# The norm between two transformer blocks folded into column factors and a row scale at evacuation; residual by column halves; last scaling shared by two engines

## The reference

```python
def rms_norm(x, g):            # first block; rms_norm_2 is the same with w
    return x * lax.rsqrt(jnp.mean(x * x, axis=-1, keepdims=True) + EPS) * g
...
x = even_layer(x, mem, ...)    # x + (y @ w_out)
x = odd_layer(x, mem, ...)     # x + (y @ w_out)
x = rms_norm(x, final_norm_g)  # end of the first block
for i in range(2):
    x = hybrid_layer(x, ...)   # h = rms_norm_2(x, norm_w[i]); ...; return x + merged @ w_out
return rms_norm_2(x, final_norm_w_2)
```

## Time and profile before

| | |
|---|---|
| median of 3 runs | 3183.61 us (3182.48 to 3185.02) |
| the profiled execution | 3181.94 us |
| its span, first to last instruction | 3179.9 us |
| PE busy | 3147.0 us, 99% |
| DVE busy | 1979.3 us, 62% |
| ACT busy | 1602.9 us, 50% |
| mean granted clock of TensorE | 0.997 |

### The profile page before, as it was taken

One profiled execution on the slowest core, in us unless ns is written; L12 is line 12 of the kernel. 1 busy time (PEld: TensorE's weight loads), 2 busy tenths in 40 slices (PEclk: granted clock), 3 DMA queues, 4 the chain that ended last, 5 costly groups with the idle time before them and its releaser, 6 DMA issues.

```text
span 3179.9 us, 38255 instructions
## 1 busy us (share of the span) xinstructions
PE 3147.0 (99%) x15096; PEld 2641.3 (83%) x15096; DVE 1979.3 (62%) x2980; ACT 1602.9 (50%) x2253; POOL 10.1 (0%) x22
## 2 busy tenths in 40 slices
PE   8999999999999999999999999999999999999998
PEld 7888888888987888888888888888888888888886
DVE  5555455565455699976555555558998655555554
ACT  7655454565454544555544444444555655444443
POOL 0000000000000000000000000000000000000000
PEclk9999999999999999999999999999999999999999
DMA  8555555545566555556566666565555466666664
GB/s 306 164 158 169 174 195 187 180 143 161 155 198 195 156 173 165 174 147 178 168 190 193 189 192 194 184 186 179 167 167 166 149 181 179 193 202 194 193 185 145
DMA packets 301442, 570.32 MB, mean 179 GB/s; under 512 B 18096, under 2 KB 36672, under 8 KB 300880
## 3 DMA queue, kind: packets, MB, share of 16 engines
q1 hardware_dynamic: 296800, 555.55, 58.2%
q10 hardware_dynamic: 3040, 6.41, 0.6%
q0 software_dynamic: 1424, 5.92, 0.5%
HBM read 565.72 MB, written 2.10 MB: 179 GB/s over the span
## 4 chain that ended last, share of the span: by engine, by line
PE 98%; DVE 1%; ACT 0%; DMA 0%; issue 0%; POOL 0%; DVEq 0%; SPq 0%
PE gp L108 90%; PE bk L108 5%; PE bk L111 3%; DVE X L139 0%; DMA raw<-in_ev_w_mem_kv 0%; DVE wl L134 0%; ACT gp L123 0%; DVE X L134 0%; DVE Hl L139 0%; ACT Yh L123 0%; DVE tmp L151 0%; ACT G L123 0%; DVE G L139 0%; ACT wh L123 0%; DVE st L134 0%
## 5 line engine op out<-in xcount | busy, mean ns | idle before, releaser
L134 DVE TENSOR_TENSOR wl<-raw,wh 128x1024 fp32r<-128x1024 f32 (+3 forms) x1088 | 1286.8, 1187 | 941.5 <-ACT wh L123 939.3
L123 ACT ACTIVATE wh<-raw 128x1024 fp32r<-128x1024 f32 (+3 forms) x1088 | 1121.4, 1034 | 1325.9 <-PE gp L108 1313.9
L108 PE MATMUL gp<-wh,Hh 128*128 128x512 f32 (+3 forms) x2400 | 925.3, 386 | 0.1
L108 PE MATMUL gp<-wh,Hl 128*128 128x512 f32 (+3 forms) x2400 | 911.9, 380 | 0.0
L108 PE MATMUL gp<-wl,Hh 128*128 128x512 f32 (+3 forms) x2400 | 911.2, 380 | 0.0
L108 PE MATMUL gp<-wh,Yh 128*128 128x512 f32 (+2 forms) x1952 | 762.0, 390 | 8.9 <-DVE wl L134 8.5
L108 PE MATMUL gp<-wh,Yl 128*128 128x512 f32 (+2 forms) x1952 | 755.2, 387 | 0.0
L108 PE MATMUL gp<-wl,Yh 128*128 128x512 f32 (+2 forms) x1952 | 754.8, 387 | 0.0
L108 PEld LDWEIGHTS gp<-wh,Hl 128*128 128x128 f32 x2400 | 451.2, 188 | 86.3
L108 PEld LDWEIGHTS gp<-wh,Hh 128*128 128x128 f32 x2400 | 451.6, 188 | 82.7 <-issue 1.3
L108 PEld LDWEIGHTS gp<-wl,Hh 128*128 128x128 f32 x2400 | 451.8, 188 | 81.3
(11 more groups left out here) (117 smaller groups left out, 1211.8 us busy)
## 6 DMA issues: line engine op xcount, KB each, us to landing
raw<-in_w_in SPq DMA_DIRECT2D x560, 512.0 KB, 3.7
raw<-in_ev_w_in SPq DMA_DIRECT2D x104, 512.0 KB, 3.8
raw<-in_od_w_in SPq DMA_DIRECT2D x80, 512.0 KB, 3.8
raw<-in_w_out SPq DMA_DIRECT2D x64, 512.0 KB, 4.7
raw<-in_ev_w_out SPq DMA_DIRECT2D x40, 512.0 KB, 3.7
raw<-in_od_w_out SPq DMA_DIRECT2D x36, 512.0 KB, 4.2
raw<-in_w_b_out SPq DMA_DIRECT2D x32, 512.0 KB, 4.6
raw<-in_w_a_out SPq DMA_DIRECT2D x32, 512.0 KB, 4.9
```

The lines of the kernel that those rows point to most:

```text
L108: return self.e.matmul(out, l, r, start=start, stop=stop)
L123: return self.e.activation(out, in_, func, **kw)
L134: return self.sketch(157 + size(a) * 1.042) if self.e is None else self.e.tensor_tensor(out, a, b, op)
```

## The change

Seven edits go together.

1. Between the blocks X is not scaled before it is used. The transposed blocks of layer 2 are made from X as the residual leaves it, part by part as for the other layers, with g·w as column factor (`gains` multiplies the two once).
2. The row scale of x2 is worked out from squares of x·g (`weigh` makes it in X) and from rs1, and `refine` multiplies rs1 into it; it acts at evacuation. `final_scale` of f0 multiplies X by rs1 later; the residual of layer 2 waits for it.
3. `residual` is two instructions of 256 columns in each row half; a `turn_in` waits for its half.
4. `mem_kv(1)` moves behind the `swkv` gemm.
5. At the end `weigh` writes X·g into M, part by part. The last scaling is a multiplication by the row scale alone: six pieces of 128x512 on DVE and two on ACT (`scale_out`).
6. Of the last part's two squares one goes to DVE (`square_last`), into `gp`, with the sum as accumulator.
7. The stores, in the order 2, 3, 0, 1, go through the queue of SP.

```diff
-         (("x", 3), 16))
+         (("x", 3), 16), (("f0",), 16))
@@ tables
-        mem_kv(1)
         W = I["od_w_in"][0]
         self.swkv = gemm(1, "H", 0, W, 1024, 256, 16, "swkv")
         roped(self.swkv, 0, 256, 64, rope_c)
         turned(self.swkv, self.swk, 0, 2)
+        mem_kv(1)
@@ sources
-            if n == 2:
-                return [self.v_fin.at((0, c))]
-            return [self.v_x.at(self.outs[n - 1][c].g)]
+            return [self.v_x.at((self.outs[n - 1][c].g, i % 4 // 2))]
@@ sp_program: store and stored moved here from pool_program
+        e.wait_ge(*P.v_fin.at((1, n)))
+        if n < 2:
+            e.wait_ge(*P.a_fin.at(n))
+        e.dma_start(o[:, :, c], P.M[:, :, c]).then_inc(*P.s_out[n].up("o", 16))
@@ act_program: in square_out
-        for t in range(2):
+        for t in range(1 if (gm.L, n) == (3, 3) else 2):
@@ act_program
+    def scale_out(n):
+        x = P.M[:, 1, 512 * n:512 * n + 512]
+        e.wait_ge(*P.v_rs.at("f1"))
+        e.wait_ge(*P.v_gf.at((1, n)))
+        e.activation(x, x, ACT.Copy, scale=P.rs[:, 1:2]).then_inc(*P.a_fin.up(n))
@@ dve_program: stat
+        if name == "x2":
+            w = P.st.buf(name)[:, 6:8]
+            e.wait_ge(*P.v_rs.at("f0"))
+            e.tensor_tensor(w, P.rs1, P.rs1, ALU.mult).then_inc(*P.v_stat.up((name, 2)))
+            e.wait_ge(*P.v_stat.at((name, 2)))
+            e.tensor_tensor(v, v, w, ALU.mult).then_inc(*P.v_stat.up((name, 3)))
@@ dve_program
-    def residual(g):
+    def residual(g, h):
...
-        x = P.X[:, :, 512 * n:512 * n + 512]
+        x = P.X[:, :, 512 * n + 256 * h:512 * n + 256 * h + 256]
...
+        if gm.L == 2:
+            e.wait_ge(*P.v_fin.at((0, n)))
+        e.tensor_tensor(x, P.gp[g % 2][:, :, 256 * h:256 * h + 256], x, ALU.add).then_inc(*P.v_x.up((g, h)))
+    def square_last(g):
+        x = P.X[:, 1, 1536:2048]
+        e.wait_ge(*P.v_x.at((g, 1)))
+        e.scalar_tensor_tensor(P.gp[g % 2][:, 1, :], x, 1.0, x, ALU.mult, ALU.mult,
+                               P.sum_x[:, 7:8]).then_inc(*P.v_sq.up(("f1", 3, 1)))
+    def weigh(f, n):
+        x, w = P.X[:, :, 512 * n:512 * n + 512], P.gfin[:, 512 * n:512 * n + 512].unsqueeze(1)
+        e.wait_ge(*P.s_gfin[f].at("g"))
+        e.wait_ge(*P.v_x.at((P.outs[1 + 2 * f][n].g, 1)))
+        if f:
+            to = P.M[:, :, 512 * n:512 * n + 512]
+            e.wait_ge(*P.p_in.at(("m", 1, 14)))
+        else:
+            to = x
+            e.wait_ge(*P.a_sq.at(("f0", n, 1)))
+            e.wait_ge(*P.p_in.at(("x", 2, 4 * n), ("x", 2, 4 * n + 2)))
+        e.tensor_tensor(to, x, w.broadcast_to([128, 2, 512]), ALU.mult).then_inc(*P.v_gf.up((f, n)))
@@ final_scale
-        for t in range(2):
-            i = e.scalar_tensor_tensor(P.X[:, t, c], P.X[:, t, c], P.rs[:, t:t + 1], P.gfin[:, c], ALU.mult, ALU.mult)
+        to, s = (P.M, P.rs) if f else (P.X, P.rs1)
+        for t in range(1 if f and n < 2 else 2):
+            i = e.tensor_scalar(to[:, t, c], to[:, t, c], s[:, t:t + 1], None, ALU.mult)
@@ add_steps
+            add("dve", "residual", g, 0)
+            add("dve", "residual", g, 1)
...
-            if gm.L in (0, 2):
+            if gm.L < 3:
...
-                for n in range(4):
+                for n in (2, 3, 0, 1):
+                    add("dve", "weigh", f, n)
+                    if not f:
+                        add("act", "square_in", "x2", n)
+                    elif n < 2:
+                        add("act", "scale_out", n)
+                if not f:
+                    norm("x2")
+                for n in (2, 3, 0, 1):
                     add("dve", "final_scale", f, n)
```

More of the change, by code:

```diff
@@ L674, in drained @@
         if gm.kind == "out":
+            if gm.L == 3 and gm.part == 3:
+                return self.v_sq.at(("f1", 3, 1))
             return self.a_sq.at((self.norm(gm.L), gm.part, 1))
@@ L810, in raw, with store, stored @@
         e.dma_start(P.raw[f % RAW][:, :, 0:gm.n], src).then_inc(*P.s_raw[f % RAW].up(f, 16))
-    return {"load_memt": load_memt, "load_mem2": load_mem2, "raw": raw}
+    def store(n):
+        o = P.out.rearrange("o (t p) c -> p (o t) c", p=128)
+        c = slice(512 * n, 512 * n + 512)
+        e.wait_ge(*P.v_fin.at((1, n)))
+        if n < 2:
+            e.wait_ge(*P.a_fin.at(n))
+        e.dma_start(o[:, :, c], P.M[:, :, c]).then_inc(*P.s_out[n].up("o", 16))
+    def stored(n):
+        e.behind("store", 1)
+        e.wait_ge(*P.s_out[n].at("o"))
+    return {"load_memt": load_memt, "load_mem2": load_mem2, "raw": raw, "store": store, "stored": stored}
 def pool_program(P, e):
@@ L853, in pad @@
         e.memset(P.glu[:, :, 0:30], 0.0).then_inc(*P.g_pad.up(l))
[L855 to L863, removed]
     return {"zero": zero, "load_constants": load_constants, "load_gfin": load_gfin, "load_second": load_second,
-            "load_cc": load_cc, "pad": pad, "store": store, "stored": stored}
+            "load_cc": load_cc, "pad": pad}
 def pe_program(P, e):
@@ L1237, in in_hi @@
             e.wait_ge(*P.s_gains.at("g"))
+            if of == ("x", 2):
+                e.wait_ge(*P.v_gains.at("x2"))
             c = P.gain_of(of) + i
@@ L1277, in root @@
         e.wait_ge(*P.v_stat.at((name, 1)))
[L1278 to L1281, removed]
+        if name in ("x1", "x2", "x3", "f1"):
+            e.wait_ge(*P.a_evac.at((P.h_end[("x1", "x2", "x3", "f1").index(name)].g, "end")))
         v = P.st.buf(name)[:, 4:6]
@@ L1400, in in_lo, with gains @@
             P.bank.give(key, P.v_in, key)
+    def gains():
+        a, b = P.gain[("x", 2)], P.gain[("f0",)]
+        e.wait_ge(*P.s_gains.at("g"))
+        e.tensor_tensor(P.gcols[:, a:a + 16], P.gcols[:, a:a + 16], P.gcols[:, b:b + 16],
+                        ALU.mult).then_inc(*P.v_gains.up("x2"))
     def stat(name):
@@ L1429, in refine @@
         i = e.tensor_tensor(out, out, t, ALU.mult)
+        if name == "x2":
+            i.then_inc(*P.v_rs.up((name, 4)))
+            e.wait_ge(*P.v_rs.at((name, 4)))
+            i = e.tensor_tensor(out, out, P.rs1, ALU.mult)
         if half is not None:
@@ L1718, in merge @@
         P.nat.give(gate, P.v_m, (g, 1))
-    def residual(g):
+    def residual(g, h):
         gm = P.gemms[g]
         n = gm.part
-        x = P.X[:, :, 512 * n:512 * n + 512]
+        if h:
+            e.behind("residual", g, 0)
+        x = P.X[:, :, 512 * n + 256 * h:512 * n + 256 * h + 256]
         e.wait_ge(*P.p_mm.at(gm.end))
@@ L1783, in add_steps @@
     add("act", "load_first")
+    add("dve", "gains")
     add("pool", "zero")
@@ L1825, in add_steps @@
                 add("pool", "load_gfin", f)
-                for n in range(4):
+                for n in (2, 3, 0, 1):
[4 more added lines that the diff above has]
+                        add("act", "scale_out", n)
+                if not f:
+                    norm("x2")
+                for n in (2, 3, 0, 1):
                     add("dve", "final_scale", f, n)
                     if f:
-                        add("pool", "store", n)
-                    else:
-                        add("act", "square_in", "x2", n)
+                        add("sp", "store", n)
                 if f:
                     for n in range(4):
-                        add("pool", "stored", n)
-                else:
-                    blocks(("x", 2), 16)
-                    norm("x2")
+                        add("sp", "stored", n)
             continue
```

48 lines of the change are left out of this document (30 added, 18 removed).

## The result

The median is 3168.17 us (3167.82 to 3168.6, 4 runs), against 3184.22 (3182.48 to 3185.02, 4 runs) for the kernel before on the same chip. That is 16.05 us less: ratio 0.995, 95% interval 0.9933 to 0.9968, so faster by more than the 0.2% that the prediction took as what can be told. The profiled execution took 3168.17 with a span of 3166.4 (before: 3181.94 and 3179.9).

The account below looks back on a forecast made before the run. PE bounds the kernel, busy 3147.0 of 3179.9 us, so only its stops and the tail count. Gains 9.2 + 2.0 + 0.6 = 11.8 us off 3183.61 give 3171.8 us, range 3168.5 to 3177.

Parts of the forecast that it names:

- The base: Starting time: the runs' median taken as 1.67 us above the profiled execution of 3181.94, so 3183.61 before the gain.
- block boundary: Stop between layers 1 and 2, about 1028 us: PE no longer waits for the scaled X, gain 9.2 us.
- inside the 9.2: At the stop between blocks, the transposes slowed by a granted clock of 0.70 were counted within the 9.2 us lost.
- The stores' queue: End of program: moving stores from POOL's queue to SP's gives between -1.5 and +0.7 us, taken as 0.3.
- first boundary: Between layers 0 and 1, about 553 us: reordering `mem_kv(1)` removes PE's stop of 2.05 us, taken as 2.0.
- rest of the tail: Tail apart from the queue: stores queued together fill the bandwidth, gain 0.3 us, bounds 0 and 0.5.
- rival C: Between layers 0 and 1: PE waits 2.6 us for late `mem` pieces and the 2.0 is not won; 3176.4, chance 0.12.
- E: Both boundaries: norm and operand work precedes weight splits in DVE's queue and PE starves 21.3 us; 3193.1, chance 0.03.
- D: Between the blocks: layer 2's input blocks still come as late as now, only 2.6 us remain; 3181.0, chance 0.05.
- The DVE square: Tail: the accumulating square on DVE takes 0.69 us plus 0.08 for reading the sum.
- rival B: Tail loses 1.3 us: accumulating square at half rate (0.5), SP landing stores late (0.8); 3173.7, chance 0.15.
- The scaling: Tail: the last scaling by row scale alone takes 0.48 us for 512 columns, against 0.75 now.

Follow-up runs that it names:

- kernel before again: The kernel before run once more with no edit; median 3184.94 us over 10 runs, ratio 1.0001.
- the `mem_kv` kernel: The kernel before with only layer 1's two `mem_kv` gemms moved behind its k/v gemm; median 3180.59 us, ratio 0.9988.
- SP stores alone: The kernel before with only its four stores and the waits for them moved from POOL's queue to SP's; median 3182.31 us, ratio 0.9995.

## Why the prediction was wrong in its size

The direction and the mechanism were right; two terms were mis-sized. Of the 3.6 us, 1.7 are in the span of the profiled execution (3166.4 for 3168.1: 1.7 from the queue, 0.3 and 0.15 from the boundaries, 0.3 in the tail's rest of that pair, less 0.8 lost at the start), 0.3 in the time outside it, and 1.67 in the base. So the time came out as near as it did partly by luck, since the profile before had a start 0.8 better than the one after.

**The base.** The step that failed is "The median of the runs is 1.67 above that execution: 3183.61 - 11.8". It took the excess of the median over the profiled execution as something that stays. The kernel before again, at its median, took 3.04 us more than that execution: 2.03 behind the stop that the change removes, 1.25 at the start, less 0.26 outside the span. The start's part stays (0.8 in the profile after); the stop's does not. The block boundary was priced at 9.2 from an execution in which the clock was back at 2.4 GHz as soon as PE resumed. The profiles gave 9.35 for it, but the folding alone took 11.7 off the median, and the scatter went from 3.4 us to 1.0. In the kernel before again 1.68 + 0.35 us were lost behind the stop at 1.2 GHz. Against executions like that the term should have been 11.0 to 11.4. The sentence that called the slower transposes "inside the 9.2" was true of that execution; it left out the slower matmuls behind them, which it did not have.

**The stores' queue.** The step is "The queue thus gives between -1.5 and +0.7; I take 0.3". It measured 2.0, outside its bounds, and is the largest single error. I had bounded it by issue and landing. Left out was the engine that waits for the last store: 0.96 us between POOL and SP. The rest, 1.09, is above the 0.7 that I took as the most. The guess of a loss of up to 1.5, from loads that land in 4.7 us, did not come about; a load's landing in mid-program says little of a store on an idle queue.

The sum with both: 11.5 (folding, without the 0.2 in its tail) + 2.3 (first boundary) + 2.0 (queue) + 0.6 (rest of the tail) = 16.4, against 16.05 measured. The difference is below what the start differs by between executions (up to 1.4 us in the profiles).

**What held.** First boundary: 2.0 forecast, 2.31 measured in both kernels; no wait near 553, no wait for `mem` pieces, so rival C fell. Block boundary in the profile: 9.2 and 9.35; no PE wait for any `lo` behind the norm work, so E fell, and D with it. Rest of the tail: 0.3 forecast with 0.5 as its bound, 0.62 measured, half of it closer packing and half an earlier first store. The DVE square: 0.69 + 0.08 forecast, 0.70 + 0.14 measured. The Trainium skill's page Vector Engine (DVE) Microarchitecture Reference, section Points that are easy to get wrong, would have it at half rate; this accumulating operation on two float32 SBUF sources (both the same piece of X) doesn't show that, and rival B lost this part as it lost the queue's. The scaling: 0.48 forecast and 0.48 measured (2.47 for six, issued 0.40 apart). The tail's stat came 0.45 later than before, 0.7 forecast, as `weigh` was put before it; the row scale 0.23 later, 0.5 forecast. The same skill's page DMA: Bandwidth & Descriptors, section Specifications, has the first byte 0.4 us sooner on SP's path; in the traces it came 0.91 us after the issue's start, against 1.29 on POOL's, so 0.38 sooner. It agrees, and is a fifth of what the queue gave.

**Parts that gave nothing or cost.** The shared square costs 0.36 as long as a `weigh` stands behind it. With the `weigh` out of the way it pays: stat then starts 2.16 us after the residual, against 2.69 with both squares on ACT and the `weigh` beside them. Moving ACT's halves is hidden by the stores; no run does without sharing the last scaling, so its worth is not shown. The residual by halves gave nothing at the block boundary, where the stretch of 2225.37 is the same with it and without. The larger gains load and the product of gains moved nothing: the first matmul starts at 8.35 against 8.49 before, and between 8.35 and 8.93 over all profiles.

**Open.** When the clock comes back after a stop of the same length differs between executions of the same program, and no run shows what decides it. How much of the 11.7 the clock made in the runs that were not profiled rests on their scatter, not on a count. Whether the stop's place in time matters (the `mem_kv` kernel) was not tried.

## What to carry to other kernels

Before taking a profiled execution as the base, set it beside the scatter of the runs: a profile at the lower end of a wide scatter may have hidden a cost, and if the change removes its cause, the median gains more than the profile. Price a stop of TensorE with the clock after it, not only its idle slots. At the end of a program, look at which engine issues the last stores and which one waits for them (2 us here, of 15), and put nothing on the engine of the last reduction that could run behind the first store (0.9 us).

## What the runs showed of the hardware

- After a stop of about 6 us and sparse transposes, matmuls ran at 1.2 GHz for some 4 us after PE was full again, in some executions; in others not at all (granted clock 0.50 and 1.00 over 1040 to 1044). The fall can come late: with 26 dummy matmuls in the stop it came at 1041.7, when PE was already busy again.
- At the start of the program the matmuls went from 0.43 to 0.23 us apart at 11.5 us in one execution and at 14.2 in another, while the granted clock read 1.00 throughout.
- A final wait on POOL ends the span 0.96 us later than one on SP, the stores being on POOL's queue in both. From the start of the last packet stored to the end of the span it was 2.3 us with stores and waits on POOL, 1.4 with the waits on SP, and 0.9 (kernel after) to 1.3 (SP stores alone) with both on SP.
- `tensor_scalar` of 128x512 float32 with a column operand took 0.48 us, the two-input forms of that size 0.69 to 0.70.
